# A two-block transformer kernel: of each pair of heads with values of their own, ScalarE scales the second head's probabilities and VectorE the first head's

## What is computed

```
s = q @ k.T + bias            # 256 x 256, causal
p = exp(s - max(s)) / sum(exp(s - max(s)))
o = p @ v
```

## Time and profile before

| | us |
|---|---|
| median of three executions | 1725.86 (1725.48 to 1728.84) |
| the profiled execution | 1723.7 |
| its span, from first to last instruction | 1721.7 |

### The profile page before, as it was taken

One profiled execution on the slowest core, in us unless ns is written; L12 is line 12 of the kernel. 1 busy time (PEld: TensorE's weight loads), 2 busy tenths in 40 slices (PEclk: granted clock), 3 DMA queues, 4 the chain that ended last, 5 costly groups with the idle time before them and its releaser, 6 DMA issues.

```text
span 1721.7 us, 29919 instructions
## 1 busy us (share of the span) xinstructions
PE 1634.9 (95%) x12199; PEld 1497.2 (87%) x12199; DVE 1134.8 (66%) x1363; ACT 792.5 (46%) x964; POOL 233.5 (14%) x300
## 2 busy tenths in 40 slices
PE   3998899998998999999999999999999999999998
PEld 2887699997876999989998978999999999889997
DVE  7787778788767544575656895555565556765554
ACT  1655433345555434454345745434453435663433
POOL 2100100000000000048947200000000002200000
PEclk9999899999999999999999999999999999999999
DMA  9874778874553655545554515555555555445552
GB/s 324 297 259 147 245 268 291 307 271 157 185 208 122 219 187 180 182 153 190 193 174 125 192 59 172 184 182 195 171 172 195 177 189 171 137 141 193 184 194 80
DMA packets 221390, 330.20 MB, mean 192 GB/s; under 512 B 6312, under 2 KB 183049, under 8 KB 221311
## 3 DMA queue, kind: packets, MB, share of 16 engines
q1 hardware_dynamic: 206112, 276.91, 48.1%
q0 software_dynamic: 14800, 52.06, 8.7%
q10 hardware_dynamic: 398, 0.11, 0.0%
HBM read 327.97 MB, written 1.09 MB: 191 GB/s over the span
## 4 chain that ended last, share of the span: by engine, by line
PE 67%; DVE 16%; ACT 6%; DMA 6%; issue 4%; SPq 0%; POOLq 0%; DVEq 0%; ACTq 0%; POOL 0%
PE bank L2367 36%; PE bank L2409 21%; DMA s_late<-in_w_ada 5%; DVE s_late L1859 4%; PE bank L2397 4%; DVE s_wL L1841 3%; ACT s_wH L1445 3%; DVE s_late L1871 2%; DMA s_mix<-in_w_ada 1%; PE bank L2379 1%; ACT s_mix L1470 1%; PE bank L2503 1%; PE bank L2466 1%; DVE s_hL L1876 1%; DVE s_mix L1927 0%
## 5 line engine op out<-in xcount | busy, mean ns | idle before, releaser
L1841 DVE TENSOR_TENSOR s_wL<-s_raw,s_wH 128x2048 fp32r<-128x2048 f32 x254 | 587.3, 2317 | 339.3 <-ACT s_wH L1445 338.6
L2367 PE MATMUL bank<-s_hH,s_wH 128*128 128x256 f32 x2240 | 636.3, 284 | 10.5 <-DVE s_hL L1889 5.2
L2367 PE MATMUL bank<-s_hH,s_wL 128*128 128x256 f32 x2240 | 633.8, 283 | 0.0
L2367 PE MATMUL bank<-s_hL,s_wH 128*128 128x256 f32 x2240 | 633.8, 283 | 0.0
L1445 ACT ACTIVATE s_wH<-s_raw 128x2048 fp32r<-128x2048 f32 x254 | 484.2, 1907 | 149.4 <-PE bank L2409 103.3
L2367 PEld LDWEIGHTS bank<-s_hH,s_wH 128*128 128x128 f32 x2240 | 429.6, 192 | 15.9 <-issue 11.6
L2367 PEld LDWEIGHTS bank<-s_hL,s_wH 128*128 128x128 f32 x2240 | 429.7, 192 | 2.3 <-issue 0.2
L2367 PEld LDWEIGHTS bank<-s_hH,s_wL 128*128 128x128 f32 x2240 | 429.6, 192 | 0.0
L2409 PE MATMUL bank<-s_wH,s_aH 128*128 128x512 f32 x496 | 195.9, 395 | 6.1 <-DVE s_aL L1964 3.7
L2409 PE MATMUL bank<-s_wL,s_aH 128*128 128x512 f32 x496 | 194.9, 393 | 0.0
L2409 PE MATMUL bank<-s_wH,s_aL 128*128 128x512 f32 x496 | 194.1, 391 | 0.0
(11 more groups left out here) (453 smaller groups left out, 2038.7 us busy)
## 6 DMA issues: line engine op xcount, KB each, us to landing
s_raw<-in_w_ffn_in SPq DMA_DIRECT2D x44, 1024.0 KB, 5.3
s_raw<-in_ffn_w_gate SPq DMA_DIRECT2D x44, 1024.0 KB, 5.2
s_raw<-in_ffn_w_up SPq DMA_DIRECT2D x44, 1024.0 KB, 5.1
s_raw<-in_ffn_w_down SPq DMA_DIRECT2D x44, 1024.0 KB, 4.8
s_late<-in_w_ada POOLq DMA_DIRECT2D x20, 2048.0 KB, 9.7
s_raw<-in_w_ffn_out SPq DMA_DIRECT2D x22, 1024.0 KB, 4.9
s_raw<-in_w_in_ab SPq DMA_DIRECT2D x12, 1024.0 KB, 9.7
s_raw<-in_w_in_cd SPq DMA_DIRECT2D x12, 1024.0 KB, 6.1
```

The costliest lines, as they stand in the source:

```text
L1841: TTn(wL[:, slot, :], raw[:, slot, :], wH[:, slot, :].bitcast(F32), ALU.subtract).then_inc(lo_ready, 1)
L2367: last = mm(dst[:, ft * T:ft * T + T], w, h[:, k, :], start=opens(name, ft, k, i), stop=(k == KC - 1 and i == 2), skip_group_check=True)
```

## The change

For a pair with values of their own (pairs 4 to 7 of ab, all of cd and of odd: 16 pairs) VectorE computes the reciprocals, tells ScalarE so on the semaphore `e_ready`, and multiplies the first head only (two instructions of four). ScalarE multiplies the second head, with two `Copy` activations whose scale is the reciprocal, in a new function `pair_scale`. `turn(p)` on TensorE now waits for both. The differential pairs stay as they were. Cut to its core:

```diff
+            def pair_scale(name, p):
+                if shared_values(name, p):
+                    return
+                act_e.wait_ge(e_ready, 3 * (PAIR0[name] + p) + 3)
+                for tt, (lo, hi) in enumerate(((0, 128), (128, 384))):
+                    last = A(sW[:, 1, lo:hi], sW[:, 1, lo:hi], ACT.Copy, scale=rs[:, 1, tt:tt + 1])
+                last.then_inc(p_ready, 1)

             def pair_normalise(name, p):
-                dve.wait_ge(e_ready, 2 * (PAIR0[name] + p) + 2)
-                step(dve.reciprocal(rs[:, 0:2, :], sums[:, 0:2, :]))
+                dve.wait_ge(e_ready, 3 * (PAIR0[name] + p) + 2)
+                dve.reciprocal(rs[:, 0:2, :], sums[:, 0:2, :]).then_inc(e_ready, 1)
+                dve.wait_ge(e_ready, 3 * (PAIR0[name] + p) + 3)
...
-                for m in range(1 if shared else 2):
-                    for tt, (lo, hi) in enumerate(((0, 128), (128, 384))):
-                        last = TS(sW[:, m, lo:hi], sW[:, m, lo:hi], rs[:, m, tt:tt + 1], None, ALU.mult)
+                for tt, (lo, hi) in enumerate(((0, 128), (128, 384))):
+                    last = TS(sW[:, 0, lo:hi], sW[:, 0, lo:hi], rs[:, 0, tt:tt + 1], None, ALU.mult)

             def pair_turn(name, p, b0, b1):
-                pe.wait_ge(p_ready, G + 1)
+                pe.wait_ge(p_ready, scaled_parts(name, p + 1))
```

ScalarE's lists call it as follows. In ab and cd, at odd s:

```diff
                     elif p >= 1:
                         pair_out(name, p - 1, 3)
+                    if s % 2:
+                        pair_scale(name, p)
                     if s in ADA_DONE[l]:
...
                 act_e.wait_ge(unit_used, n0 + 11 + USED0 + 1)
+                pair_scale(name, 6)
                 if l == 0:
                     upper_turned(1)
...
                 pair_probs(name, 7)
+                pair_scale(name, 7)
                 pair_direct(name, 6, 6, 3).then_inc(oh_ready, 1)
```

In odd:

```diff
             evacuate(6, v, 0)
             q_copy(1, 0)
+            pair_scale("odd", 0)
             pair_copy("odd", 0, 6, 7)
...
             evacuate(7, v, 1)
+            pair_scale("odd", 1)
             pair_copy("odd", 1, 6, 7)
...
             split_py(n0 + 10)
+            pair_scale("odd", 2)
...
             pair_probs("odd", 3)
+            pair_scale("odd", 3)
```

More of the change, by code:

```diff
@@ L249, in copies, with scaled_parts @@
         def copies(name, p):
+            return {"ab": p if p <= 4 else 2 * p - 4, "cd": 12 + 2 * p, "odd": 28 + 2 * p}[name]
+        def scaled_parts(name, p):
             return {"ab": p if p <= 4 else 2 * p - 4, "cd": 12 + 2 * p, "odd": 28 + 2 * p}[name]
@@ L999, in odd_pe, with odd_act @@
             out_half(3, 1)
-        def odd_act(act_e, A, step, split_py, row_copy, pair_probs, pair_copy, pair_out, pair_direct):
+        def odd_act(act_e, A, step, split_py, row_copy, pair_probs, pair_scale, pair_copy, pair_out, pair_direct):
             n0, o0, G0 = START["odd"], START["o_odd"], PAIR0["odd"]
@@ L1822, in _ @@
                 else:
-                    odd_act(act_e, A, step, split_py, row_copy, pair_probs, pair_copy, pair_out, pair_direct)
+                    odd_act(act_e, A, step, split_py, row_copy, pair_probs, pair_scale, pair_copy, pair_out, pair_direct)
                 sqrt_table()
```

## The result

| | before | after |
|---|---|---|
| median of five executions each | 1725.86 (1724.47 to 1731.24) | 1739.94 (1738.36 to 1742.86) |
| ratio, 95% interval | | 1.0076 [1.0055, 1.0096] |
| the profiled execution | 1723.7 | 1739.9 |
| its span | 1721.7 | 1738.0 |
| mean granted clock | 0.992 | 0.985 |

What follows compares the result with a forecast made beforehand. TensorE, 67% of the span, bounds the kernel, so softmax counts only where TensorE waits. ab 0.55 + cd 1.57 + clock 1.25 + odd 3.76 = +7.1 us, median 1733.0 us (+0.4%), range 1729.5 to 1736.0.

Steps and rivals of the forecast that it cites:

- The gain at cd's turns: cd, pairs 1, 3 and 5: each turn begins 0.43 us earlier, TensorE 1.10 us ahead in all, absorbed before the projection.
- ScalarE's queue is late for odd's `turn(0)` and `turn(1)`: odd, pairs 0 and 1: a new wait of 2.57 us at the first turn, +3.76 us with the second.
- the evacuation and split behind the scaling push cd's projection: cd, end of the steps: the chain from pair 5's reciprocal starts the output projection 1.57 us later.
- the sum for pair 1 of odd: odd, pair 1: turn at 1498.67 instead of 1494.91 after ScalarE's evacuation and scaling, +3.76 us with the first wait.
- The scale from a pointer costs nothing visible: Each new ScalarE pair takes 0.60 us to its end, 0.51 us of the queue, with 0.84 us as upper bound.
- I see nothing else late: cd, from its output projection to its end: TensorE's own work and short chains set the pace, no further delay.
- my 5.9: The sum of the forecast in us without the clock loss in cd.
- The clock: cd, behind the new 3.5 us wait before the projection: granted clock falls to about half, costing +1.25 us.
- the clock is down there already: ab, behind the wait before its projection: the projection starts 0.55 us later, with no clock loss added.
- The clock falls in odd too: Rival: odd's 2.57 us wait at `turn(0)` also lowers the clock, some 1.2 us more, 8.4 in all, 1734.2; chance 0.20.
- More than 10 us: Case: the change costs over 10 us through a slower scaling (0.84 us and up) or an unfound wait; chance 0.04.

Runs made afterwards that it cites:

- cd alone: ScalarE scales the second head in cd only, VectorE multiplies all four in ab and odd as before: 1731.54 us, ratio 1.0031 to the kernel before.
- the last column of the table: Stretch lengths, changed kernel against kernel before, both with TensorE multiplying zeros during waits: 0.76 and 1.71 in ab, 2.33 and 0.86 in cd, 4.23 in odd, sum 9.9 us.
- with products: Products of zeros added on TensorE during its waits: to the changed kernel, 1732.62 us, ratio 1.0037; to the kernel before, 1724.81 us, ratio 0.9996.

## Why the prediction was right and wrong

- **Direction and places: right.** The gain at cd's turns is small and is lost again; ScalarE's queue is late for odd's `turn(0)` and `turn(1)`; the evacuation and split behind the scaling push cd's projection. The order of the links in the timeline is that of the text. Two slips in it change nothing: the sum for pair 1 of odd comes to 1498.64, not 1498.67, and in ab `turn(3)` does wait for its probabilities, 2.23 us, but that is a differential pair, which the change leaves alone.
- **"The scale from a pointer costs nothing visible": wrong.** It costs 0.09 us a copy, 0.18 a pair. The row that I cited for it, two copies with such a scale in 0.84 us, has the cost in it; I read it as an upper bound and took the plain copies for the sum. What failed is a term's size: each turn in cd gained 0.21 instead of 0.43, so that by pair 5 TensorE was 0.27 us ahead (cd alone), not 1.10, and the scaling stands twice in the chain to the projection. Together: 2.64 instead of 1.57 in cd, 0.77 instead of 0.55 in ab, 0.3 more at odd's `turn(0)`. With a constant scale all three are within 0.11 us of the forecast. Against the last column of the table this is 1.4 us of what was missing.
- **"I see nothing else late" behind cd's projection: wrong.** `turn(7)` waits for pair 6's output behind `pair_scale(7)`, in ab and cd, 1.2 and 0.7 us once the clock is up; the two stretches that hold it are 1.71 and 0.86 us longer with products, where the forecast had nothing but clock. That is 2.6 us. These two points make 9.9 us out of my 5.9 in the stretches, 7.8 by the medians.
- **The clock: the term that was most in error.** I took 1.25 us, in cd alone, and wrote for ab that "the clock is down there already". It was, for 3 us; with the longer wait it stayed down for 9. In odd I gave its fall a chance of 0.20; it fell for 3 us behind the wait of 2.70 us, some 1.5 us. The table without products, less its last column, gives what the change adds: 1.2 to 1.4 us in ab, 2.2 to 2.3 in cd and 1.6 in odd, 5.0 to 5.3 in all, where I had 1.25; by the medians it is 6.3. In ab the changed kernel loses 2.6 us to the clock, but the kernel before loses 1.4 there too; the other 1.7 of the 2.95 is the delay at `turn(7)`, which the slow clock hides and which stands there once the clock is up.
- **The rivals.** "The clock falls in odd too" was the right one for odd, and at 1734.2 the nearest of them. "More than 10 us", at 0.04, is what came, through a slower scaling and a wait that I had not found, as it said; but about half of what was missing is the clock (4 of 8 us in the stretches, 5 of 7 by the medians). The range reached 3 us above the forecast and had no case in which the clock costs more than 2.5.
- The Trainium skill (TensorE: Matmul & The Clock Gate, What's actually happening) has the half clock as the default state, released by activity, and says that the number of slow matmuls at a kernel's start differs between runs of the same kernel. By that rule both new waits could cost, and the traces agree: the clock was 0.50 behind both. In mid-kernel too the length differed, 3 and over 8 us behind the same 3.72 us.

## What to carry to other kernels

Before work goes to an idle engine, look at what stands behind it in that engine's list: here 0.46 us less on VectorE was paid with an evacuation and a split that now wait for the reciprocal, and of the two places tried for it in cd neither was free. Price an instruction from a row with the same kinds of operands, not only the same shape. And where TensorE's wait grows by a microsecond, count the clock as a term of its own, also where the clock was low before: here waits that grew by 1.0, 2.9 and 2.7 us were followed by 1.2 to 1.4, 2.2 and 1.6 us of it. A version in which TensorE multiplies zeros during the wait measures that term, best by stretches, since the clock elsewhere differs from one execution to the next.

## What the runs showed of the hardware that I had not expected

- A scale that is read from memory lengthens an activation by 0.09 us (387 for 295 ns with 128 columns, 506 for 418 with 256); 8 partitions (292 and 399 ns) or 128 (295 and 418) make next to none.
- Behind one and the same wait of 3.72 us the granted clock stayed at 0.50 for 3 us in one trace and over 8 us in another, of the same instructions; behind cd's wait of 3.73 us, for 3 us in the first trace of the change and some 6 us in the second and with cd alone.
- A wait of 1.74 us on TensorE (pair 3 in the kernel with the scaling behind the split) was followed by a clock of 0.84 and 0.59 in the next 6 us, while waits of the same length at pairs 1 and 5 of that trace were not followed by a lower clock. Why is open.
- A semaphore signal that ScalarE gave by itself, not with an activation, arrived ahead of activations that stand before it in the list: odd's `turn(0)` began at 1490.90 us, the evacuation ahead of the signal at 1491.54. `turn(0)` had no wait in that kernel, and one of 2.70 us with the signal on the copies.
